# A two-block network on one core: where neighbourhood attention starts beside the recurrence

## The chip, the cores and the metric

One core of a Trainium2 chip runs the whole program. The metric is the device time of one execution in microseconds; the time before is the median of three runs. Engines in the rows: PE is TensorE's matmuls, PEld its weight loads, DVE VectorE, ACT ScalarE, POOL GpSimd, SP SyncE, which issues all DMAs.

## The reference, cut to what matters

Two blocks over 256 tokens of width 1024, all in 32-bit floats. The first block (attention, a state-space mixer, a layer of experts) and the second block's convolutions and feed-forward layers are not touched. The change lies in the even mixer of the second block, which joins two parts:

```python
def even_mixer(h, h_ctx, ...):
    na_q, na_k, na_v, hg_q, hg_ff, hg_fb, hg_i, hg_g = split(h @ w_in)      # and the same of h_ctx
    a_lat = neighbourhood_attention(na_q, na_k, na_v, cna_k, cna_v, rpb)    # 8 heads of 64
    g_lat = hgrn2_mixer(hg_q, (hg_ff, hg_fb), hg_i, hg_g, ...)              # 4 heads of 128
    return concatenate([a_lat, g_lat]) @ w_out

# HGRN2: a recurrence over 8 chunks of 32 tokens, forwards and backwards
o         = qe @ state + (causal part inside the chunk)
new_state = exp(btot) * state + kd.T @ v
# readout, per head
o = o * rsqrt(mean(o * o) + eps) * norm_w * silu(g)
```

Neighbourhood attention of a head: scores of 256 queries against 256 tokens (with a bias) and 256 tokens of context, a softmax, and the weighted sum of values.

## The kernel before, in words

`build` writes one program for each engine (`pe`, `act`, `dve`, `pool`, `sp`). The order on an engine is that of its own Python code; engines meet through semaphores. Code that is to run beside other code is a generator, and `next` puts its next piece into the program at that place, so the order is written out by hand, once for each engine.

Every weight tile of 128x1024 is a unit of a stream. SP loads it, ACT rounds it to a high part (line 1077), DVE subtracts to get a low part (line 1528), and PE makes three products per 128 rows (lines 376 to 378). ACT and DVE call `halves` and `lows` ahead of each wait, so that they work up to `AHEAD` = 3 units in front of PE.

PE's results go to eight PSUM banks. `Banks.take` goes round them in program order of PE and leaves out those that are still held (taken, and not marked full). Whoever takes a bank waits until its last user's data have been read (`is_empty`). So an insertion in PE's order changes which tile later shares a bank with which.

The stage of the change, in PE's order:

1. `recurrence()` (from line 907 on): transposes, the causal part, and then 16 half steps, n = 0 to 7 by direction d. A half step has four state products (`sd`, line 948, only for n < 7) and four output products (line 954) into the banks o0 and o1, which are held until the last half step. DVE does two operations on the state for each (lines 2108 and 2112).
2. `quarters()` (line 968 on): four tiles of weight products are cut into four quarters each, 16 in all, one ahead of each of the 16 half steps. The tiles are named in `QUARTERS`: `("ek", 3)`, the last keys of attention, `("eq", 1)`, the last queries, `("hg", 0)` and `("hg", 1)`, the gate. ACT takes each out of its bank in `tile_out` (line 1340 for eq, 1342 for ek, 1344 for hg with silu).
3. `neighbourhood()`: 16 turns n (head and half of the queries), two yields each, "half turns" 2n and 2n+1. PE: score n (line 877), turned product n-2 (line 868: transposes the probabilities and scales them by a diagonal matrix of reciprocal sums), in the second half valued n-3 (line 887) into a bank `nav` for four turns each. DVE: bias, copy and maximum (lines 2066, 2067, 2069), in the second half the reciprocal and the diagonal of turn n-1 (lines 2074, 2078). ACT: at turns 7, 11, ... the copy of a value tile (line 1402), then copy n-2 of the turned product (line 1407), and the exponential with its sum (line 1414), all ahead of both yields.
4. The heads' readout of the recurrence lies beside attention. DVE copies o out of o0 and o1 (line 2116), ACT squares it (1446), DVE multiplies by the gate (2130), PE sums (`head_mean`, line 999), ACT takes the root (1450), DVE the reciprocal (2134), PE spreads it over two banks os0 and os1 (`head_rows`, line 1008), DVE multiplies (2140), ACT and DVE split the result (1455, 2121). In `act` and `dve` these steps are the generator `heads()`, one `next` per turn; in `pe` they stand at half turns 3 and 7.
5. From half turn 20 on every second half turn carries a half tile of the output projection (`mixer_out`), which needs the readout's results.

Of the kernel before, what the change touches and what calls it, by code (L numbers as in the profile page):

```python
# [155 lines left out]
def build(nc, D, out):  # L156
# [8 lines left out]
    with es:  # L165
# [31 lines left out]
        B = Banks(ps, S)  # L197
# [58 lines left out]
        eq, lists = view(arp, 80, 128, 16), view(scp, 0, 3, 256)  # L256
# [82 lines left out]
        def run(steps):  # L339
            for _ in steps:  # L340
                pass

        VROWS, QUARTERS, HEADS = (0, 3, 6, 9), [("ek", 3), ("eq", 1), ("hg", 0), ("hg", 1)], range(20, 36, 2)

        NORMS = ["n1", "n2", "nc", "l0", "f0", "od", "f1", "fin"]
        RES = {"n2": 0, "l0": 3, "f0": 7, "od": 11, "f1": 14, "fin": 17}
# [21 lines left out]
        def pe(e):  # L370
            t = Eng(e)
# [490 lines left out]
            def neighbourhood():  # L862
                def turned(n):
                    P = take(("nt", n))
                    i = n % 3
                    t.wait_ge(S["n_diag"], n + 1)
                    for k in range(4):
                        last = mm(P[:, k * 128:k * 128 + 128], nP[:, i, k * 128:k * 128 + 128], nD[:, i, :], start=True, stop=True)  # L868
                    last.then_inc(B.full(("nt", n), len(W.units)), 1)

                def scored(n):
                    h, qt = n // 2, n % 2
                    j, b0 = h // 2, 64 * (h % 2)
                    P = take(("ns", n))
                    t.wait_ge(*B.is_empty(("eq", 1)))
                    t.wait_ge(*B.is_empty(("ek", 3)))
                    mm(P[:, :], nq[b0:b0 + 64, j, qt * 128:qt * 128 + 128], nk_[b0:b0 + 64, j, :], start=True, stop=True).then_inc(
                        B.full(("ns", n), len(W.units)), 1)

                def valued(n):  # L880
                    h, qt, i = n // 2, n % 2, n % 3
                    b0 = 64 * (h % 2)
                    P = B[("nav", n // 4)] if n % 4 else take(("nav", n // 4))
                    t.wait_ge(*B.is_empty(("nt", n)))
                    t.wait_ge(*B.is_empty(("nv", 3)))
                    for k in range(4):
                        last = mm(P[b0:b0 + 64, qt * 128:qt * 128 + 128], nv[:, k, h * 64:h * 64 + 64],
                                  nT[i][:, k * 128:k * 128 + 128], start=k == 0, stop=k == 3)
                    if n % 4 == 3:
                        last.then_inc(B.full(("nav", n // 4), len(W.units)), 1)  # L890
                    else:
                        last.then_inc(S["n_part"], 1)
                for n in range(19):
                    if n < 16:
                        scored(n)
                    if 2 <= n < 18:
                        turned(n - 2)
                    yield
                    if n >= 3:
                        valued(n - 3)  # L900
                    yield
# [64 lines left out]
                next(hgr)  # L966
            run(nv_rows)
            W.mark("bias")
            for key in QUARTERS:
                for _ in quarters(key, "ev_" + {"ek": "k", "eq": "q"}.get(key[0], "hg"), key[1] if key[0] == "ek" else 2 * key[1],  # L970
                                  (XA, XC) if key[0] == "ek" else None):
                    next(hgr)


            def cat(k):
# [33 lines left out]
                                  start=True, stop=True)  # L1009
                    last.then_inc(B.full(("os", q), len(W.units)), 1)  # L1010
            heads = (step for i in range(4) for step in mixer_out(i, 1))
            for n, _ in enumerate(neighbourhood()):
                if n == 3:
                    head_mean()
                if n == 7:
                    head_rows()
                if n in HEADS:
                    next(heads)
# [45 lines left out]
        def act(e):  # L1064
# [272 lines left out]
            def tile_out(name, i):  # L1337
                P = bank((name, i))
                if name == "eq":
                    nc.scalar.mul(flat(nq[:, 2 * i:2 * i + 2, :]), P[:, :], 0.125).then_inc(B.empty((name, i)), 1)  # L1340
                elif name == "ek":
                    put(nk_[:, i, :], P[:, :], ACT.Copy).then_inc(B.empty((name, i)), 1)
                else:
                    put(flat(hg[:, 2 * i:2 * i + 2, :]), P[:, :], ACT.Silu).then_inc(B.empty((name, i)), 1)
# [73 lines left out]
            def recurrence():  # L1418
# [15 lines left out]
                for d in range(2):  # L1434
                    P = bank(("s0", d))
                    put(SS[:, d, 0].rearrange("p h v -> p (h v)"), P[:, :], ACT.Copy).then_inc(B.empty(("s0", d)), 1)
                    yield
            run(recurrence())
            for key in QUARTERS:
                tile_out(*key)  # L1440

            def heads():
                for q in range(2):
                    two = slice(2 * q, 2 * q + 2)
                    a.wait_ge(*B.is_empty(("o", q)))
                    put(sq4[:, two], oT[:, two], ACT.Square).then_inc(S["o_sq"], 1)
                yield
                yield
                P = bank("head_stat")
                put(root8, P[:, 0:8], ACT.Sqrt, bias=eps).then_inc(B.empty("head_stat"), 1)  # L1450
                yield
                yield
                for h in range(4):
                    a.wait_ge(*(B.is_empty(("os", h // 2)) if h % 2 else (S["og"], h // 2 + 1)))
                    put(XC[0][:, 4 + h], oT[:, h, :], ACT.Copy).then_inc(S["cat_hh"], 1)
                    if h % 2:
                        yield
            hs = heads()
            for n, _ in enumerate(neighbourhood()):
                if n % 2 == 0:  # L1460
                    next(hs, None)
            run(hs)
# [52 lines left out]
        def dve(e):  # L1515
# [565 lines left out]
            def recurrence():  # L2081
                for s in range(2):
                    for d in range(2):
                        for hf in range(2):
                            lows(B.units[("kt", s, d, hf)] + AHEAD)
                v.wait_ge(*B.is_full(("kt", 1, 1, 1)))
                fill(flat(attT), 0.0).then_inc(own.up(), 1)
                v.wait_ge(own.sem, own.n)
                v.wait_ge(S["ld_hm"], 16)
                for d in range(2):  # L2090
                    for hf in range(2):
                        P = bank(("at", d, hf))
                        nc.vector.copy_predicated(attT[:, d * 8 + hf * 4:d * 8 + hf * 4 + 4, :],
                                                  hm[:, d, :].bitcast(i32).unsqueeze(1).to_broadcast([128, 4, 128]),
                                                  P[:, :].rearrange("p (a b) -> p a b", b=128)).then_inc(B.empty(("at", d, hf)), 1)
                        yield
                for d in range(2):
                    lows(B.units[("s0", d)] + AHEAD)
                for n in range(8):
                    for d in range(2):  # L2100
                        c = n if d == 0 else 7 - n
                        if n < 7:
                            s0, s1 = SS[:, d, n % 2], SS[:, d, (n + 1) % 2]
                            v.wait_ge(S["ebt"], d + 1)
                            v.wait_ge(*B.is_empty(("sd", n - 1, d) if n else ("s0", d)))
                            if n:
                                v.wait_ge(S["o_part"], 2 * (n - 1) + d + 1)
                            tt_(s1, s0, ebt[:, d, :].rearrange("p (h c) -> p h c", c=8)[:, :, c:c + 1].to_broadcast([128, 4, 128]),
                                ALU.mult).then_inc(own.up(), 1)
                            P = bank(("sd", n, d))  # L2110
                            v.wait_ge(own.sem, own.n)
                            tt_(s1, s1, P[:, :].rearrange("p (h v) -> p h v", v=128), ALU.add).then_inc(B.empty(("sd", n, d)), 1)
                        yield
                for q in range(2):
                    v.wait_ge(*B.is_full(("o", q)))
                    copy(flat(oT[:, 2 * q:2 * q + 2, :]), B[("o", q)][:, :]).then_inc(B.empty(("o", q)), 1)
                yield

            def cat_lo(h):
                v.wait_ge(S["cat_hh"], h + 1)  # L2120
# [4 lines left out]
            def heads():  # L2125
                for q in range(2):
                    two = slice(2 * q, 2 * q + 2)
                    v.wait_ge(S["o_sq"], q + 1)
                    v.wait_ge(*B.is_empty(("hg", q)))
                    tt_(oT[:, two], oT[:, two], hg[:, two], ALU.mult).then_inc(S["o_gate"], 1)  # L2130
                yield
                yield
                v.wait_ge(*B.is_empty("head_stat"))
# [12 lines left out]
                    if h % 2:  # L2146
                        yield
            hs = heads()
            for n, _ in enumerate(neighbourhood()):
                if n % 2:  # L2150
                    next(hs, None)
            run(hs)
# [306 lines left out]
```

## Time and profile before

| | |
|---|---|
| median of three runs | 2152.5 us (2150.4 to 2155.31) |
| the profiled execution | 2151.5 us, span 2149.7 us |
| busy: PE, PEld | 98%, 94% of the span |
| busy: DVE, ACT, POOL | 73%, 52%, 12% |
| chain that ended last, by engine | PE 75%, DVE 17%, ACT 4%, DMA 2%, issue 2% |

A row by stretch gives its length, then the busy time of PE, PEld, DVE, ACT and POOL with the number of instructions, then PEclk (TensorE's granted clock as a share of the full 2.4 GHz; 0.50 is 1.2 GHz), the share of the DMA engines' time, and GB/s. A row of a timeline gives start and length in us, engine, line, operation, output and inputs by name with the shape, the count of instructions merged, and in brackets the engine's idle time before it with what ended it. Lengths of neighbouring matmuls overlap a little, so what a piece costs PE is read from one start to the next.

### The profile page before, as it was taken

Reading aid. Unit: us, or ns where it says so; the run is one execution under the profiler, and the core shown is the slowest. Engines: PE = TensorE matmul, PEld = TensorE weight load, DVE = VectorE, ACT = ScalarE, POOL = GpSimd, SP = SyncE. Lnnn points to the kernel's source line nnn. Section 1 sums busy time; section 2 is a strip of 40 time slices with the busy share of each in tenths; the row PEclk is TensorE's granted clock in tenths of the full one; section 3 lists DMA queues with packets and bytes.
Section 4 is the critical chain, followed back from the end, with each engine's and each line's share of the span. In section 5 each row is a group of like instructions: output and inputs, shape, how many; then the busy total and the mean of one; then the engine's idle time right before and its main releaser. Section 6 shows DMA issues by size and latency. Waiting matters only on the chain.

```text
span 2149.7 us, 40331 instructions
## 1 busy us (share of the span) xinstructions
PE 2099.5 (98%) x16798; PEld 2026.2 (94%) x16798; DVE 1565.5 (73%) x2758; ACT 1122.4 (52%) x1745; POOL 261.2 (12%) x256
## 2 busy tenths in 40 slices
PE   7999999999999999999999999999999999999998
PEld 7899998999999999999999999999878999999998
DVE  6877688775999777877777677564455887877764
ACT  5566677545444666654444445463245554445553
POOL 0000000002887445410000000000000000000000
PEclk9999999999999999999999999999989999999999
DMA  5543433567555444447667767322103777655553
GB/s 193 167 135 115 150 118 118 195 217 245 187 187 168 147 145 141 138 165 243 230 236 277 250 226 246 128 89 108 35 20 129 253 248 251 236 193 170 185 181 122
DMA packets 104293, 375.43 MB, mean 175 GB/s; under 512 B 11568, under 2 KB 12208, under 8 KB 103728
## 3 DMA queue, kind: packets, MB, share of 16 engines
q1 hardware_dynamic: 104112, 372.86, 51.6%
q8 instruction: 133, 2.18, 0.4%
q14 instruction: 48, 0.39, 0.1%
HBM read 370.71 MB, written 2.10 MB: 173 GB/s over the span
## 4 chain that ended last, share of the span: by engine, by line
PE 75%; DVE 17%; ACT 4%; DMA 2%; issue 2%; SPq 0%; DVEq 0%; ACTq 0%
PE ps L376 20%; PE ps L377 19%; PE ps L378 19%; DVE wl L1528 3%; PE ps L770 3%; DVE arenap L1870 2%; ACT wh L1077 1%; DVE arena L1671 1%; DMA raw<-in_ada 1%; PE ps L564 1%; PE ps L462 1%; DVE arenap L1835 1%; PE ps L463 1%; PE ps L464 1%; PE ps L868 1%
## 5 line engine op out<-in xcount | busy, mean ns | idle before, releaser
L376 PE MATMUL ps<-xah,wh 128*128 128x256 f32 x2800 | 798.7, 285 | 2.6 <-DVE wl L1528 1.0
L377 PE MATMUL ps<-xal,wh 128*128 128x256 f32 x2800 | 787.5, 281 | 0.0
L378 PE MATMUL ps<-xah,wl 128*128 128x256 f32 x2800 | 786.9, 281 | 0.0
L1077 ACT ACTIVATE wh<-raw 128x1024 fp32r<-128x1024 f32 (+1 forms) x608 | 620.6, 1036 | 296.6 <-PE ps L378 153.6
L1528 DVE TENSOR_TENSOR wl<-raw,wh 128x1024 fp32r<-128x1024 f32 (+2 forms) x548 | 644.6, 1197 | 175.6 <-ACT wh L1077 174.2
L376 PEld LDWEIGHTS ps<-xah,wh 128*128 128x128 f32 x2800 | 528.6, 189 | 13.1 <-issue 5.8
L377 PEld LDWEIGHTS ps<-xal,wh 128*128 128x128 f32 x2800 | 528.8, 189 | 0.5 <-issue 0.2
L378 PEld LDWEIGHTS ps<-xah,wl 128*128 128x128 f32 x2800 | 528.5, 189 | 0.0
L376 PE MATMUL ps<-hh,wh 128*128 128x256 f32 x1024 | 291.1, 284 | 6.8 <-DVE wl L1528 5.1
L377 PE MATMUL ps<-arenar,wh 128*128 128x256 f32 x1024 | 288.7, 282 | 0.0
L378 PE MATMUL ps<-hh,wl 128*128 128x256 f32 x1024 | 288.7, 282 | 0.0
L2255 POOL TENSOR_TENSOR wl<-raw,wh 128x1024 fp32r<-128x1024 f32 x60 | 145.9, 2439 | 553.7 <-ACT wh L1077 553.6
L376 PEld LDWEIGHTS ps<-hh,wh 128*128 128x128 f32 x1024 | 194.2, 190 | 8.5 <-DVE wl L1528 6.5
L377 PEld LDWEIGHTS ps<-arenar,wh 128*128 128x128 f32 x1024 | 194.3, 190 | 0.0
L378 PEld LDWEIGHTS ps<-hh,wl 128*128 128x128 f32 x1024 | 194.1, 190 | 0.0
L2262 POOL TENSOR_SCALAR hh<-cst,scp 128x128 fp32r<-128x128 f32 x192 | 115.1, 618 | 120.2 <-PE ps L770 120.2
L376 PE MATMUL ps<-xfh,wh 128*128 128x256 f32 x416 | 118.1, 284 | 2.3 <-DVE wl L1528 2.1
L378 PE MATMUL ps<-xfh,wl 128*128 128x256 f32 x416 | 117.6, 283 | 0.0
L377 PE MATMUL ps<-xfl,wh 128*128 128x256 f32 x416 | 117.5, 283 | 0.0
L1288 ACT ACTIVATE hh<-arenap 128x256 fp32r<-128x256 f32 x128 | 52.5, 411 | 108.0 <-PE ps L378 108.0
L1910 DVE TENSOR_TENSOR arenar<-arenap,hh 128x256 fp32r<-128x256 f32 x128 | 53.3, 421 | 67.1 <-ACT hh L1288 66.3
L1624 DVE SCALAR_TENSOR_TENSOR scp<-raw,small,scp 128x512 f32<-128x512 f32 x112 | 80.4, 749 | 27.3 <-DMA raw<-in_ada 25.8
(351 smaller groups left out, 3132.2 us busy)
## 6 DMA issues: line engine op xcount, KB each, us to landing
raw<-in_pu SPq DMA_DIRECT2D x128, 512.0 KB, 3.4
raw<-in_pv SPq DMA_DIRECT2D x128, 512.0 KB, 3.7
raw<-in_ada SPq DMA_DIRECT2D x96, 512.0 KB, 4.3
raw<-in_ff_up SPq DMA_DIRECT2D x88, 512.0 KB, 4.2
raw<-in_w_xbc SPq DMA_DIRECT2D x32, 512.0 KB, 3.3
raw<-in_ff_down SPq DMA_DIRECT2D x32, 512.0 KB, 4.0
raw<-in_w_z SPq DMA_DIRECT2D x16, 512.0 KB, 3.2
raw<-in_w_so SPq DMA_DIRECT2D x16, 512.0 KB, 3.9
```

The source lines that it names most:

```text
L376: mm(o, w0, x0, start=start, stop=False, skip_group_check=skip)
L377: mm(o, w0, x1, start=False, stop=False, skip_group_check=skip)
L378: return mm(o, w1, x0, start=False, stop=stop, skip_group_check=skip)
L770: last = mm(P[:, a * 128:a * 128 + 128], o[:, a, :].bitcast(f32), o2[:, a, :], start=True, stop=True)
L1077: put(W.hi(i), W.raw(i), ACT.Copy).then_inc(S["high"], 1)
L1288: put(hh[:, n % 4, :], HA[:, n, :], ACT.Copy).then_inc(S["h_hi"], 1)
L1528: tt_(W.lo(i), W.raw(i), W.hi(i).bitcast(f32), ALU.subtract).then_inc(S["lowV"], 1)
L1624: stt(dst, wv[:, kk, :], by, dst, ALU.mult, ALU.add).then_inc(step[0], 1)
L1870: last = stt(e4[:, :, :, j], p3, float(j), if16[:, tt, s, :, j:j + 1].to_broadcast([128, 8, 16]), ALU.is_equal, ALU.mult)
L1910: tt_(har[n // 32][:, n % 32, :], HA[:, n, :], hh[:, n % 4, :].bitcast(f32), ALU.subtract).then_inc(S["h_lo"], 1)
L2255: nc.gpsimd.tensor_tensor(W.lo(i), W.raw(i), W.hi(i).bitcast(f32), ALU.subtract).then_inc(S["lowG"], 1)
L2262: last = nc.gpsimd.tensor_scalar(ones1[g % 2][:, a, :], iota, lists[:, 0, 4 * g + a:4 * g + a + 1], None, ALU.is_equal)
```

## The change

`QUARTERS` puts the gate's tiles hg 0 and hg 1 ahead of ek 3 and eq 1. PE issues scores 0 and 1 beside the last two half steps, and score 0 waits only for the tiles with its own head's queries and keys. DVE does maxima 0 and 1 and diagonal 0 ahead of the copies of o; ACT does exponentials 0 and 1 ahead of the copy of eq 1. The remaining turns are counted from 3 (PE, ACT) or 4 (DVE). On PE the heads' mean moves from half turn 3 to 5 and the heads' rows from 7 to 9; in `act` and `dve` the first piece of `heads()` now stands ahead of the turns, and one more `yield` follows it.

```diff
-        ... QUARTERS, ... = ..., [("ek", 3), ("eq", 1), ("hg", 0), ("hg", 1)], ...
+        ... QUARTERS, ... = ..., [("hg", 0), ("hg", 1), ("ek", 3), ("eq", 1)], ...
@@ pe: scored(n)
-                    t.wait_ge(*B.is_empty(("eq", 1)))
-                    t.wait_ge(*B.is_empty(("ek", 3)))
+                    t.wait_ge(*B.is_empty(("eq", j // 2)))
+                    t.wait_ge(*B.is_empty(("ek", j)))
@@ pe
+            near, done = neighbourhood(), 0
             for key in QUARTERS:
                 for _ in quarters(key, ...):
+                    if done == 14:
+                        next(near)
+                    elif done == 15:
+                        next(near)
+                        next(near)
                     next(hgr)
+                    done += 1
...
-            for n, _ in enumerate(neighbourhood()):
-                if n == 3:
+            for n, _ in enumerate(near, 3):
+                if n == 5:
                     head_mean()
-                if n == 7:
+                if n == 9:
                     head_rows()
@@ act
+            near = neighbourhood()
             for key in QUARTERS:
+                if key == QUARTERS[3]:
+                    for _ in range(3):
+                        next(near)
                 tile_out(*key)
@@ act: heads(), behind the squares, and dve: heads(), behind the gate
+                yield
                 yield
                 yield
@@ act
             hs = heads()
-            for n, _ in enumerate(neighbourhood()):
+            next(hs)
+            for n, _ in enumerate(near, 3):
                 if n % 2 == 0:
                     next(hs, None)
@@ dve: recurrence()
-                for n in range(8):
+                for n in range(7):
...
+                for _ in range(4):
+                    next(near)
                 for q in range(2):
                     v.wait_ge(*B.is_full(("o", q)))
                     copy(flat(oT[:, 2 * q:2 * q + 2, :]), B[("o", q)][:, :]).then_inc(B.empty(("o", q)), 1)
@@ dve
             hs = heads()
-            for n, _ in enumerate(neighbourhood()):
+            next(hs)
+            for n, _ in enumerate(near, 4):
                 if n % 2:
                     next(hs, None)
```

## Rows read from the trace of the kernel before

**Rows 1.** Busy time by stretch; PEclk is TensorE's granted clock, 1.00 full.
```profile
1552.00:1576.00 24.00, 21.59 (x90) 15.17 (x90) 12.40 (x31) 11.45 (x21) 0.00 (x0) 0.72 0.03 11
```

**Rows 2.** Order of time, PE, around the change: start, length, instruction, idle before.
```profile
1549.47 0.97 PE L954 MATMUL ps<-arena 128*128 128x32 f32 x8
...
1551.79 0.97 PE L954 MATMUL ps<-arena 128*128 128x32 f32 x8
1553.10 1.98 PE L877 MATMUL ps<-arena 64*128 64x512 f32 x4 [0.34 <-DVE arena L2116]
1557.15 3.58 PE L999 MATMUL ps<-J,arena 128*128 128x1 f32 x16 [2.08 <-ACT arena L1446]
1560.66 2.07 PE L877 MATMUL ps<-arena 64*128 64x512 f32 x2
1562.66 2.07 PE L868 MATMUL ps<-sc,arena 128*128 128x128 f32 x8
...
1568.67 1.80 PE L887 MATMUL ps<-arena 128*64 128x128 f32 x8
1570.40 2.05 PE L1008 MATMUL ps<-cst,small 128*128 128x128 f32 x16
1572.38 1.12 PE L877 MATMUL ps<-arena 64*128 64x512 f32 x2
1573.43 1.16 PE L868 MATMUL ps<-sc,arena 128*128 128x128 f32 x8
1574.52 1.09 PE L887 MATMUL ps<-arena 128*64 128x128 f32 x8
1575.54 1.12 PE L877 MATMUL ps<-arena 64*128 64x512 f32 x2
```

**Rows 3.** Busy time by microsecond, columns as in rows 1.
```profile
957.00:958.00 1.00, 0.14 (x2) 0.00 (x0) 0.21 (x1) 0.82 (x2) 0.00 (x0) 1.00 0.09 33
958.00:959.00 1.00, 0.12 (x1) 0.15 (x2) 1.00 (x3) 1.00 (x2) 0.00 (x0) 1.00 0.85 262
...
1556.00:1557.00 1.00, 0.00 (x0) 0.00 (x0) 0.00 (x0) 1.00 (x3) 0.00 (x0) 0.75 0.00 0
...
1570.00:1571.00 1.00, 1.00 (x8) 0.83 (x8) 0.00 (x0) 0.99 (x2) 0.00 (x0) 0.92 0.00 0
```

**Rows 4.** The page: the splits of weights on DVE, count, busy, mean ns.
```profile
L1528 DVE TENSOR_TENSOR wl<-raw,wh 128x1024 fp32r<-128x1024 f32 (+2 forms) x548 | 644.6, 1197 | 175.6 <-ACT wh L1077 174.2
```

**Rows 5.** The same stretch on DVE.
```profile
1552.35 1.29 DVE L2116 COPY arena<-ps 128x512 f32<-128x512 f32 x2 [4.51 <-PE ps L954]
...
1554.26 0.42 DVE L2066 TENSOR_TENSOR arena<-ps,arena 128x256 f32<-128x256 f32 x1
...
1555.05 0.69 DVE L2069 TENSOR_REDUCE sc<-arena 128x1 f32<-128x512 f32 x1
1557.13 1.29 DVE L2130 TENSOR_TENSOR arena<-arena 128x512 f32<-128x512 f32 x2 [1.40 <-ACT arena L1446]
...
1567.68 0.20 DVE L2134 RECIPROCAL small<-small 128x8 f32<-128x8 f32 x1 [3.04 <-ACT small L1450]
...
1575.12 0.29 DVE L2078 TENSOR_SCALAR sc<-cst,sc 128x128 f32<-128x128 f32 x1
1575.32 0.87 DVE L2140 SCALAR_TENSOR_TENSOR arena<-arena,pcol,ps 128x256 f32<-128x256 f32 x2
```

**Rows 6.** The same stretch on ACT.
```profile
1551.99 0.60 ACT L1344 ACTIVATE arena<-ps 128x512 f32<-128x512 f32 x1 [5.23 <-PE ps L378]
...
1555.77 0.72 ACT L1414 ACTIVATE arena<-arena,sc 128x512 f32<-128x512 f32 x1 [1.89 <-DVE sc L2069]
...
1556.49 1.13 ACT L1446 ACTIVATE arena<-arena 128x512 f32<-128x512 f32 x2
...
1566.08 1.28 ACT L1450 ACT_TABLE_LOAD   x1
1567.38 0.27 ACT L1450 ACTIVATE small<-ps,small 128x8 f32<-128x8 f32 x1
```

More of the change, by code:

```diff
@@ L341, in run @@
                 pass
-        VROWS, QUARTERS, HEADS = (0, 3, 6, 9), [("ek", 3), ("eq", 1), ("hg", 0), ("hg", 1)], range(20, 36, 2)
+        VROWS, QUARTERS, HEADS = (0, 3, 6, 9), [("hg", 0), ("hg", 1), ("ek", 3), ("eq", 1)], range(20, 36, 2)
         NORMS = ["n1", "n2", "nc", "l0", "f0", "od", "f1", "fin"]
@@ L2117, in recurrence @@
                 yield
+            near = neighbourhood()
             def cat_lo(h):
@@ L2130, in heads @@
                     tt_(oT[:, two], oT[:, two], hg[:, two], ALU.mult).then_inc(S["o_gate"], 1)
+                yield
                 yield
```

## The prediction

> **What bounds the kernel now.** I read the page first: PE is busy in 98% of the span and DVE in 73%, so only places where PE waits, or runs slowly, can give time back. The place the diff touches is the seam between the gated recurrence and neighbourhood attention. The stretch view [rows 1] says what is wrong there: in 24 us PE is busy for 21.59 us, and its mean granted clock is 0.72. The timeline of PE [rows 2] gives the reason. After the recurrence's last matmuls (1551.79) PE waits 0.34 us for bank o0, which DVE still copies out, runs two scores (two records each) up to 1555.08, and then stands 2.08 us before the heads' mean (line 999), because ACT squares o (line 1446) behind the first exponential. In that idle time the clock falls from full to half, in the microsecond with a mean of 0.75 [rows 3]; it is full again early in the one with 0.92. From 1557.15 on, a score takes 2.00 us instead of 1.05 and a turned product 2.0 instead of 1.09 (starts [rows 2]).
>
> So the seam costs, against a PE that never stops: 0.34 + 2.08 = 2.4 us idle, and the half clock. From 1557.15 to 1572.38 there are 15.2 us of work. At full clock it is: mean 1.8 (half of 3.5), two scores at 1.05, two turned at 1.09, one valued at 1.02, head rows 1.98, together 9.1. The half clock costs 6.2 us, the seam 8.6. That is the most this change can win, 0.4% of the kernel.
>
> **The change part by part.** Half turn k below is the k-th yield of the neighbourhood generator (turn n has 2n and 2n+1). All times are on the axis of the trace.
>
> *Order of the quarter tiles.* The same products and the same seven weight units; the first four are split before the quarters begin, ek's and eq's follow beside the products of hg, in gaps that ACT and DVE have there as before. 0.0 us. If that cover were gone, PE would wait for one split on DVE, 1.2 us [rows 4]. The bias load stands before the same seventh unit, so it stays early.
>
> *Scores 0 and 1.* They slip between PE's last pieces. From 1549.47 to 1551.79 there lie one o product and one quarter tile, 2.32 us [rows 2], which I part as 0.81 and 1.51. Score 0 begins at 1549.47, o ends 1551.33, the last quarter 1552.84, score 1 ends 1553.9, the last o 1554.7, score 2 ends 1555.8. No wait: by the rotation of the eight banks (o0 and o1 are still held) the scores now take banks emptied long ago. The 0.34 us goes. DVE finds score 0 at 1550.6; a maximum is ready 1.48 us after its score (1554.26 to 1555.74 [rows 5]), an exponential 0.8 us later (0.72 [rows 6] and the read of its sum). Maximum 1 is out at 1555.45, diagonal 0 at 1555.9 [rows 5].
>
> *Wait 1, new.* The rotation gives turned product 0 the bank of the tile eq 1. ACT now empties that tile behind exponential 1: 1555.5 + 0.8, then 0.60 for the copy [rows 6], done at 1556.85. PE stands from 1555.8 to 1556.9: **1.1 us**. Behind it on ACT are the squares (1.13 [rows 6]), ready at 1558.0, just when turned 0 ends. So the heads' mean in its new place waits for nothing: the 2.08 us goes.
>
> *Wait 2, new.* The mean and the rows move by two half turns on PE (3 to 5, 7 to 9). On ACT the root moves from half turn 4 to 8, on DVE the reciprocal from 5 to 9: two generator steps are gone to the front and one yield is added, and each step is two half turns. So the root now stands behind exponential 4, whose score is PE's last but two. At full clock: score 4 ends 1564.0, maximum 1565.5, ACT copies turned 2 (until 1565.75), exponential 1566.6, table load 1.28, root 0.27 [rows 6], reciprocal 0.20 [rows 5]: 1568.35. PE has turned 2 and valued 1 to do, until 1566.1, and then stands **2.3 us** (between 2.0 and 2.5, by how the copy falls). Before, the same chain was ready at 1567.88, 2.5 us ahead of line 1008.
>
> The Trainium skill, "ScalarE: Activation LUTs", section "What ACT_TABLE_LOAD costs", gives a switch of tables about 2.66 us, the load and a drain behind it. In this trace the root starts 0.02 us after a load of 1.28 us has ended [rows 6]; by the page wait 2 would be 3.7 us instead of 2.3, and the sum below +4.9 us. I go by the row.
>
> *Wait 3, new.* The rotation of the banks gives the second value tile of attention (valued 4, turn 7) the bank of the second head rows. DVE empties that bank in line 2140, which has moved from half turn 11 to 15, behind turn 7's maximum and diagonal. From score 7's end: maximum 1.48, reciprocal and diagonal 0.45, line 2140 0.87 [rows 5], 2.8 us, against 1.09 us of PE's turned 5: 1.7 us at least. ACT adds to it: its two copies of o (0.8) now stand ahead of the copy of value tile 0, for which DVE's queue waits ahead of maximum 7. I take **2.2 us**, between 1.7 and 2.9.
>
> Waits: 1.1 + 2.3 + 2.2 = 5.6 us instead of 2.4. So the change moves PE's idle time apart, and more than doubles it; what it can win lies in the clock.
>
> *The clock.* The rows show no simple price. PE stood 1.7 us in 957 to 959 [rows 3], between dense products, and the clock stayed full. At 1555.08 it stood 2.08 us and the clock fell, after two scores that use 64 rows of the array. In the new order the stretch from 1552.84 to 1559.8 holds two scores, one o product with 32 columns a matmul, one turned product, the mean with one column in each of its matmuls, and 1.1 us idle: hardly more work for PE than in the stretch where it fell. I take it that the clock falls there again, near 1556.5, and is back at about 1570.1 as before. Then: turned 0 from 1556.9 to 1558.9, mean to 1562.4, score 3 to 1564.4, turned 1 to 1566.4, valued 0 to 1568.15, score 4 to 1570.15, turned 2 and valued 1 at full clock to 1572.25. The root's chain from score 4 ends 4.1 us after it, at 1574.25, so wait 2 is 2.0 us; head rows to 1576.2. Score 5 starts at 1576.2 where it started at 1575.54: 0.7 us late. With wait 3 and an uncertain 0.6 for ACT's and DVE's fuller turn 7, the sum is **+3.5 us** (0.7 + 2.2 + 0.6). Ends of this case: +1.9 if the clock is back earlier (at 1566.7), +5.5 if later or with wait 3 at its upper bound.
>
> The profiled execution took 2151.5 us (span 2149.7), 1.0 below the median of the three runs, 2152.5. I put the sum on the median: 2156.0.
>
> **The rivals.**
> 1. *The clock stays full at the seam.* For it: PE's longest gap there shrinks from 2.08 to 1.1 us, and 1.7 us cost nothing at 957. Against: the thin matmuls around it. Then 6.2 us of half clock go, and idle time grows by 3.2: -3.0 us, 2149.5.
> 2. *The clock falls a second time, in wait 2 or wait 3 (slower).* Place: 1566 to 1568, or turn 7. Both gaps are as long as the one that let it fall before, and nothing dense stands beside wait 3. Price: one more half-clock stretch of 3.4 to 6.8 us (half or a quarter of the 13.6 us from 1556.5 to 1570.1 [rows 3]), half of that lost, 1.7 to 3.4, on top of +3.5: about +6.5, 2159.0. It decides as soon as PE's wait before the head rows or before valued 4 is over 2 us. The Trainium skill, "TensorE: Matmul & The Clock Gate", section "A second HAM failure mode: psum-queue depth-cycling", says that a PE which keeps stopping shortly between groups of matmuls, as it goes round the PSUM banks, can let its clock swing between the levels. By that rule this rival is the likeliest outcome, at its 2159.0; the trace of before agrees once (2.08 us) and disagrees once (1.7 us).
> 3. *The new waits are not there or are short*, because an engine is quicker than I have it or the bank order differs: 8.6 less 1.1 to 3 us, about -6.5, 2146.0. For it: a large part of the 8.6 is real. Against: the half turns are written in the code.
> 4. *Nothing to see:* gain and waits cancel, 2152.5.
>
> **How the numbers follow.** About 0.2% (4.3 us) is what a measurement of this kernel can tell from no change. Forecast 35%, rival 1 20%, rival 2 27%, rival 3 10%, rival 4 8%. Faster by over 0.2% (under 2148.2): rival 3 and a part of rival 1, 0.15. Slower (over 2156.8): rival 2 but for a little, and the upper third of the forecast, 0.38. The rest, 0.47, is within. Range: from rival 1's 2149.5 less 1 to rival 2's 2159 plus 2.5, 2148.5 to 2161.5; what is left out is rival 3 and the tail of rival 2.
>
> **What would show each step.** PE has no wait between the last quarter and score 2. ACT's copy of eq 1 ends before turned 0 starts, with a PE wait of about 1.1 us released by ACT's line of that copy. The line of the head rows waits for DVE's reciprocal, 2 us or more. Valued 4 waits for DVE's line 2140 (its number after), about 2 us. PEclk between 1553 and 1576 is at 0.5 for about 13 us. I am wrong if it stays at 1.0 there, if head rows or valued 4 wait for nothing, or if the clock is at 0.5 anywhere in turns 5 to 10.

## The result and the profile after

| | changed | before | ratio, 95% interval |
|---|---|---|---|
| first comparison (6 runs each) | 2157.88 us | 2152.32 us | 1.0027 (1.0015 to 1.0039) |
| second, later (10 and 27 runs) | 2157.28 us | 2152.22 us | 1.0031 (1.0019 to 1.0043) |
| profiled execution, span | 2155.5 us | 2149.7 us | |

The change costs 5 to 6 us by the medians, 0.3% (by the two intervals together, 3 to 9 us). The forecast was 2156.0, +3.5. Of all executions one, of kernel 2 below, took 5224 us; its ratio leaves it out, and the median of 2147.90 given there would be 2147.51 without it.

All three new waits are there. PE after the change, in order of time (to compare with [rows 2]; this kernel reached its quarter tiles 1.3 us earlier, at 1496.34 instead of 1497.66):

```profile
1551.80 1.12 PE L877 MATMUL ps<-arena 64*128 64x512 f32 x2
1552.85 1.08 PE L954 MATMUL ps<-arena 128*128 128x32 f32 x8
1553.86 1.12 PE L877 MATMUL ps<-arena 64*128 64x512 f32 x2
1555.82 1.75 PE L868 MATMUL ps<-sc,arena 128*128 128x128 f32 x8 [0.84 <-ACT arena L1347]
1557.35 3.41 PE L1006 MATMUL ps<-J,arena 128*128 128x1 f32 x16
1560.69 2.07 PE L877 MATMUL ps<-arena 64*128 64x512 f32 x2
...
1566.55 1.12 PE L877 MATMUL ps<-arena 64*128 64x512 f32 x2
...
1568.69 1.09 PE L887 MATMUL ps<-arena 128*64 128x128 f32 x8
1572.06 2.64 PE L1015 MATMUL ps<-cst,small 128*128 128x128 f32 x16 [2.28 <-DVE small L2152]
1574.63 2.07 PE L877 MATMUL ps<-arena 64*128 64x512 f32 x2
...
1580.35 1.12 PE L877 MATMUL ps<-arena 64*128 64x512 f32 x2
...
1584.56 1.16 PE L868 MATMUL ps<-sc,arena 128*128 128x128 f32 x8
1587.95 1.09 PE L887 MATMUL ps<-arena 128*64 128x128 f32 x8 [2.23 <-DVE arena L2158]
1588.97 1.12 PE L877 MATMUL ps<-arena 64*128 64x512 f32 x2
```

The waits of 0.34 and 2.08 us are gone. In their place stand 0.84 us before turned product 0, released by ACT's copy of eq 1 (L1347), 2.28 us before the head rows (L1015), released by DVE's reciprocal (L2152), and 2.23 us before valued 4, released by the products of the readout (L2158). Why the first is there and the second is so long can be read on ACT. The copy of eq 1 starts behind exponential 1 (the read of its sum). Exponential 4, the table load and the root follow each other directly:

```profile
1555.10 0.19 ACT L1421 ACTIVATION_READ_ACCUMULATOR arena<-arena,sc 128x1 f32 x1
1555.19 0.58 ACT L1347 ACTIVATE arena<-ps 128x512 f32<-128x512 f32 x1
...
1569.30 0.71 ACT L1421 ACTIVATE arena<-arena,sc 128x512 f32<-128x512 f32 x1
1569.91 0.19 ACT L1421 ACTIVATION_READ_ACCUMULATOR arena<-arena,sc 128x1 f32 x1
1570.12 1.28 ACT L1462 ACT_TABLE_LOAD   x1
1571.41 0.27 ACT L1462 ACTIVATE small<-ps,small 128x8 f32<-128x8 f32 x1
```

The third can be read on DVE, where value tile 0 (L2074), maximum 7 and its diagonal stand ahead of the second pair of products:

```profile
1584.92 0.42 DVE L2074 TENSOR_TENSOR xcl<-ps,xch 128x256 fp32r<-128x256 f32 x1 [0.75 <-ACT xch L1409]
1585.26 0.42 DVE L2079 TENSOR_TENSOR arena<-ps,arena 128x256 f32<-128x256 f32 x1
...
1586.83 0.29 DVE L2091 TENSOR_SCALAR sc<-cst,sc 128x128 f32<-128x128 f32 x1
1587.03 0.87 DVE L2158 SCALAR_TENSOR_TENSOR arena<-arena,pcol,ps 128x256 f32<-128x256 f32 x2
```

PEclk, last column but two, by microsecond, answers to [rows 3]:

```profile
1556.00:1557.00 1.00, 1.00 (x7) 1.00 (x7) 0.71 (x3) 0.80 (x2) 0.00 (x0) 0.60 0.00 0
...
1566.00:1567.00 1.00, 1.00 (x5) 0.56 (x4) 0.00 (x0) 0.10 (x2) 0.00 (x0) 0.78 0.00 0
...
1573.00:1574.00 1.00, 1.00 (x8) 1.00 (x7) 0.00 (x0) 0.00 (x0) 0.00 (x0) 0.64 0.00 0
...
1580.00:1581.00 1.00, 1.00 (x5) 0.47 (x3) 0.00 (x0) 0.99 (x2) 0.00 (x0) 0.95 0.00 0
```

A mean of 0.60 in a microsecond is a fall after its first fifth. So the clock is at half from 1556.2 to 1566.4 and again from 1573.3 to 1580.1, just after the long wait before the head rows: 17.1 us instead of 13.7. The second fall is the one of rival 2. The last wait, 2.23 us before valued 4, is not followed by one.

### The profile page after: what moved, and what is told of

The parts are those of the page before. It is cut to its first block, busy times and chain, and to the rows that moved or that the text cites. A ratio compares the mean times of both kernels' runs of the same rounds, so it can differ in the third digit from the quotient of the medians.

```text
span 2155.5 us, 40333 instructions
## 1 busy us (share of the span) xinstructions
PE 2099.1 (97%) x16798; PEld 2025.3 (94%) x16798; DVE 1565.8 (73%) x2758; ACT 1123.0 (52%) x1745; POOL 261.1 (12%) x256
## 4 chain that ended last, share of the span: by engine, by line
PE 73%; DVE 17%; ACT 5%; DMA 2%; issue 2%; SPq 0%; DVEq 0%; ACTq 0%
PE ps L376 19%; PE ps L377 19%; PE ps L378 19%; DVE wl L1541 3%; PE ps L770 3%; DVE arenap L1883 2%; ACT wh L1084 2%; DVE arena L1684 1%; DMA raw<-in_ada 1%; PE ps L564 1%; PE ps L462 1%; DVE arenap L1848 1%; PE ps L463 1%; PE ps L464 1%; DVE arenap L1843 1%
```

## The experiments

The median moves by whatever the clock does in other stages as well: by the mean clocks of the profiles, 26 to 38 us at half clock lie outside the seam. So I also read one length in each profile: from the first quarter tile to the start of score 11, behind the seam. "Idle" is the sum of PE's waits of over 0.15 us in it, "half" the time at half clock, "added" the time of products that compute nothing, and "rest" is length - idle - half/2 - added. Every profile also has one wait of 0.93 us before score 11; it is the same in all and stays in "rest".

One profile is one execution. The last column takes all of them: the time that a whole execution lost to the clock, (1 - its mean granted clock) x its span, as the mean over a kernel's executions, and in brackets the same of the kernel before measured beside it. It is worked out from clocks given to three digits; the standard error is about 0.4 us for the kernel before and 0.5 to 1.3 for the others.

| | length | idle | half | added | rest | lost, all executions (before) |
|---|---|---|---|---|---|---|
| before | 99.24 | 2.42 | 13.7 | 0 | 90.0 | 22.9, 23.6 and 23.7 |
| changed | 104.52 | 5.35 | 17.1 | 0 | 90.6 | 26.7 (23.7) |
| root earlier | 95.09 | 0.84 | 6.8 | 0 | 90.9 | 22.7 (22.9) |
| and eq 1 first | 93.18 | 0.20 | 3.4 | 0 | 91.3 | 19.1 (22.9); once more 19.3 (23.7) |
| order alone | 97.94 | 2.42 | 10.2 | 0 | 90.4 | 23.4 (22.9) |
| before, gap filled | 94.35 | 0.34 | 0.0 | 3.2 | 90.8 | 18.2 (22.9) |
| products late | 105.12 | 3.07 | 23.9 | 0 | 90.1 | 25.1 (23.6) |
| changed, rows' gap filled | 104.35 | 3.07 | 13.7 | 3.9 | 90.5 | 23.1 (23.6) |
| mean later | 97.95 | 2.10 | 10.2 | 0 | 90.8 | 25.0 (23.6) |
| eq 1 first, mean filled | 97.13 | 0.00 | 10.2 | 1.3 | 90.7 | 17.8 (23.6) |
| the same once more | 95.60 | 0.00 | 6.8 | 1.3 | 90.9 | 17.9 (23.7) |

Changed and eq 1 first were profiled twice (second time 104.53 with 17.1, and 91.59 with 0.0 of half clock; rest 90.6 and 91.4). The rest stays within 1.4 us, so idle time and half clock explain nearly all of the differences at this place. Half/2 is a rough price: before, the clock fell 0.64 us ahead of the end of the idle time (1556.51, against 1557.15), and half clock in idle time costs nothing, so the rest of before is nearer 90.3.

All executions of the second comparison agree with the table: the changed kernel's mean is 5.9 us above the other's (2158.0 and 2152.1), of which 3.0 is the clock and 2.9 is not, and the profiles have 2.93 us more idle time.

**1. Root earlier** (the changed kernel without its added yields):

```diff
@@ act: heads(), behind the squares, and dve: heads(), behind the gate
-                yield
                 yield
                 yield
```

> The changed kernel, but ACT's and DVE's heads() have no added yield, so the root stands behind exponential 3 instead of 4 and line 2158's two pairs of products (the old 2140) at half turns 11 and 13 instead of 13 and 15. Theory (the loss is the two waits that the half turns make, 2.28 us before the head rows and 2.23 us before valued 4, and the second fall of the clock in the first of them, 6.8 us at half clock = 3.4 us): both waits are gone, the clock falls once at the seam, 8 us less than the changed kernel, about 2150. Rival A (the loss is in starting the scores early, by the wait for the tile eq 1 and a longer mean): the time stays within 2 us of the changed kernel, 2156 to 2158. Rival B (the clock's swings have nothing to do with these waits): only 4.5 us come back, 2153.4, and the clock still falls twice.

Measured: 2151.31 us, before 2151.57, ratio 1.0000 (0.9991 to 1.0009). PE of this kernel at the head rows and at valued 4:

```profile
1569.37 1.09 PE L887 MATMUL ps<-arena 128*64 128x128 f32 x8
1570.38 2.05 PE L1015 MATMUL ps<-cst,small 128*128 128x128 f32 x16
...
1579.73 1.16 PE L868 MATMUL ps<-sc,arena 128*128 128x128 f32 x8
1580.82 1.09 PE L887 MATMUL ps<-arena 128*64 128x128 f32 x8
```

Neither has a wait, and the clock falls once. One `yield` in each of two engines' programs is the whole loss of the change. Rivals A and B are out. The profile's seam is 4.2 us shorter than before, which the times do not show. Most of that is the profile's half clock, 6.8 us instead of 13.7, and over all executions the clock takes as much as before (22.7 and 22.9 us): this profile had luck with the clock. What the early scores win in idle time, 1.6 us less 0.9 of rest, is within the interval.

**2. Eq 1 first** (on top of 1):

```diff
@@ act
                 if key == QUARTERS[3]:
-                    for _ in range(3):
-                        next(near)
+                    next(near)
+                    next(near)
                 tile_out(*key)
+            next(near)
```

> As the kernel with the root earlier, and ACT copies the tile eq 1 between exponentials 0 and 1 instead of behind both. Theory: turned 0 waits only for its diagonal, the 0.84 us wait before it shrinks to about 0.1 us; the squares are ready no sooner, so PE waits up to 0.8 us before the heads' mean instead. The gain over the kernel with the root earlier is 0 to 0.8 us: about 2149.8. Rival (the wait before turned 0 is what lets the clock fall at 1556): the clock stays full at the seam and 4 to 6 us more come back, 2144 to 2146.

Measured: 2146.41 us, before 2151.57, ratio 0.9980 (0.9970 to 0.9990); once more 2147.90 against 2152.22, 0.9982 (0.9973 to 0.9991). The rival came closer in time, though its clock stayed full in one of two profiles only. Just 0.6 us of idle time went, yet the ratio is 0.2% better than the last one's. The clock accounts for most of it: in the two profiles 3.4 and 0.0 us at half clock are left, and over all executions 19.1 us are lost instead of 22.7.

```profile
1555.18 1.13 PE L868 MATMUL ps<-sc,arena 128*128 128x128 f32 x8
1556.35 1.95 PE L1006 MATMUL ps<-J,arena 128*128 128x1 f32 x16
1558.23 1.12 PE L877 MATMUL ps<-arena 64*128 64x512 f32 x2
1559.55 2.01 PE L868 MATMUL ps<-sc,arena 128*128 128x128 f32 x8 [0.20 <-DVE sc L2091]
```

Turned 0 and the mean follow score 2 with hardly a gap, and the clock (a turned product is 2.01 us again) falls only behind the mean and score 3. In the second profile it does not fall here at all.

**3. Order alone** (the kernel before with the new `QUARTERS`):

> The kernel before with the order of the quarter tiles of the change alone (hg 0, hg 1, ek 3, eq 1), scores where they were. Theory: nothing, 2152.3 within 1.5 us; PE has the same 0.34 and 2.08 us waits at the seam. Rival (a wait for a late weight split or for the last tiles of attention moves into the quarters): 1 to 3 us slower, with a wait inside the 16 quarters.

Measured: 2152.62 us, before 2151.57, 1.0006 (0.9997 to 1.0015), waits of 0.34 and 2.08 us as before. Nothing, as expected.

**4. The gap before the mean filled, in the kernel before:**

```diff
@@ pe: head_mean()
                 P = take("head_stat")
+                keep(P, 14)
```

> The kernel before with 14 products of the identity with itself (128 columns, into unused columns of the mean's bank) ahead of the wait for the heads' mean, some 1.9 us of dense work in its 2.08 us gap. Theory (6.2 us of the seam are half clock, caused by that gap): the clock stays full, scores take 1.05 us, and the time falls by 5 to 6 us less what DVE and ACT then hold up, 2146 to 2149. Rival (the thin matmuls of the mean with one column each let the clock fall even without a gap): the clock falls at the seam all the same, a step later at most, and the time is within 2 us of 2152.3.

Measured: 2148.70 us, before 2151.57, ratio 0.9985 (0.9976 to 0.9994).

```profile
1557.19 3.39 PE L476 MATMUL ps<-cst 128*128 128x128 f32 x28
1560.42 1.84 PE L1000 MATMUL ps<-J,arena 128*128 128x1 f32 x16
1562.20 1.12 PE L877 MATMUL ps<-arena 64*128 64x512 f32 x2
1563.25 1.16 PE L868 MATMUL ps<-sc,arena 128*128 128x128 f32 x8
```

Useless work in the gap makes the kernel faster: score and turned product behind it take 1.05 and 1.09 us, and the clock never leaves 1.00 in this seam; over all executions 18.2 us are lost to it instead of 22.9. I had the 14 products at 1.9 us; they take 3.2 (two records each), so 1.15 us of them is past the gap's end. So the gap is what let the clock fall in this seam: filled with dense products, it did not. That a gap is needed for a fall is not shown, and kernel 8 below speaks against it.

**5. Products late** (as 1, but the added yield behind the root and the reciprocal): the wait of valued 4 by itself.

```diff
@@ act and dve: heads(), against the changed kernel
-                yield
                 yield
                 yield
                 ... the root; the reciprocal ...
                 yield
                 yield
+                yield
```

> The changed kernel with the added yield of heads() in ACT and DVE put behind the root and the reciprocal instead of ahead of them: the root stands behind exponential 3, the two pairs of products stay at half turns 13 and 15. Theory (the two waits are separate; the one before the head rows, with the second fall of the clock, costs 5.7 us, the one before valued 4 costs 2.2): the wait before the head rows is gone, valued 4 still waits 1.7 to 2.3 us, one fall of the clock; the time is 2.2 us above the kernel with the root earlier (2151.3), about 2153.5. Rival (a gap of 2.2 us in thin work always lets the clock fall): it falls again behind valued 4 and the time is 2155 to 2157.

Measured: 2155.17 us, before 2152.51, ratio 1.0017 (1.0006 to 1.0028).

```profile
1583.04 1.16 PE L868 MATMUL ps<-sc,arena 128*128 128x128 f32 x8
1586.43 1.36 PE L887 MATMUL ps<-arena 128*64 128x128 f32 x8 [2.23 <-DVE arena L2158]
1587.72 2.07 PE L877 MATMUL ps<-arena 64*128 64x512 f32 x2
1589.72 2.08 PE L868 MATMUL ps<-sc,arena 128*128 128x128 f32 x8
```

PE has the 2.23 us before valued 4 and then runs at half clock (a score 2.00 us again). Against kernel 1 (1.0000) the one wait costs 0.17% or 3.7 us, 1.4 more than its length; the intervals are too wide to tell that surplus by time, but the profile shows the fall. The rival came true here: this gap too can let the clock fall. It does not always, since the changed kernel's two profiles have the same wait and no fall.

**6. Head rows' gap filled, in the changed kernel:**

```diff
@@ pe: head_rows()
                 for q in range(2):
                     P = take(("os", q))
+                    if q == 0:
+                        keep(P, 17)
                     t.wait_ge(S["rstd8"], 1)
```

> The changed kernel with 17 products of the identity with itself ahead of the wait for the head rows' reciprocal, 2.1 us of dense work in the 2.28 us gap; all three waits keep their ends. Theory (the second fall of the clock, 6.8 us at half clock, costs 3.4 us by itself, and idle time calls it): one fall at the seam, none at 1573; the head rows start when they did, and the time is 3.0 us less, about 2154.9. Rival (the second fall costs nothing, since DVE and ACT are late at that place anyway): the clock stays full and the time stays at 2157.9.

Measured: 2155.74 us, before 2152.51, ratio 1.0025 (1.0011 to 1.0039), which overlaps the changed kernel's own: undecided by time.

```profile
1568.65 4.06 PE L476 MATMUL ps<-cst 128*128 128x128 f32 x34
1572.55 1.95 PE L1017 MATMUL ps<-cst,small 128*128 128x128 f32 x16
...
1585.19 1.47 PE L887 MATMUL ps<-arena 128*64 128x128 f32 x8 [2.23 <-DVE arena L2160]
1586.59 2.07 PE L877 MATMUL ps<-arena 64*128 64x512 f32 x2
```

The 17 products take 3.9 us, 1.6 more than the gap, so the head rows did not start when they had. In the profile the clock does not fall there, as the theory has it, but it falls behind valued 4 (at 1585.7), where it had stayed full in the changed kernel.

**7. Mean later** (on top of 2):

```diff
@@ pe
-                if n == 5:
+                if n == 6:
                     head_mean()
```

> The kernel with eq 1 copied between the exponentials (2146.4), and PE's heads' mean at half turn 6 instead of 5, behind score 3 and turned 1. Theory (what lets the clock fall there is thin work side by side: scores, the last o product, and the mean's one-column products with a short wait): with denser pieces around the mean the clock stays full in most runs, 1 to 2 us less, 2144.5 to 2145.5. Rival (ACT's root then waits for the mean and holds up the copy of turned 2): a new wait of 0.5 to 1 us before valued 1 or the head rows, the clock as before, 2147.

Measured: 2151.92 us, before 2152.51, 1.0002 (0.9993 to 1.0012). Both were wrong.

```profile
1558.64 1.12 PE L877 MATMUL ps<-arena 64*128 64x512 f32 x2
1561.86 1.16 PE L868 MATMUL ps<-sc,arena 128*128 128x128 f32 x8 [2.10 <-DVE sc L2091]
```

Turned 1 now stands where the mean was and waits 2.10 us for DVE's diagonal 1, which stands behind the copies of o, the gate and maximum 2. In kernel 2 the mean covers that time. Its place was right. Behind this wait the clock falls for 10.2 us in the profile.

**8. Mean filled** (on top of 2):

```diff
@@ pe: head_mean()
                 P = take("head_stat")
+                keep(P, 6)
```

> The kernel with eq 1 copied between the exponentials (2146.4), with 6 products of the identity ahead of the heads' mean, 0.8 us of dense work where PE has almost no gap. Theory (one stretch of 3.4 us at half clock is left there and costs 1.7 us): the clock stays full, 1.7 us come back and 0.8 are paid, 2145.5. Rival (the mean itself is thin enough): the clock falls all the same and the time is 0.8 us more, 2147.2.

Measured: 2147.74 us, before 2152.51, ratio 0.9971 (0.9961 to 0.9982).

```profile
1562.76 1.12 PE L877 MATMUL ps<-arena 64*128 64x512 f32 x2
1563.81 1.32 PE L868 MATMUL ps<-sc,arena 128*128 128x128 f32 x8
1565.06 1.97 PE L887 MATMUL ps<-arena 128*64 128x128 f32 x8
```

The theory's "the clock stays full" did not hold in the profile: it falls at 1564.7 for 10.2 us, and PE has no wait of over 0.15 us ahead of it in the seam. In the second profile of this kernel (below) it falls twice, at 1557.9 and 1564.7, for 3.4 us each, again without such a wait. Both profiled executions took more than their medians (2150.98 and 2152.20 us), and over all executions this kernel loses least to the clock, 17.8 and 17.9 us.

The last three runs, all on one chip:

> The changed kernel once more, beside the two below on one chip. Theory: 5.6 us above the kernel before, 2157 to 2159. Rival (its first six runs were unlucky with the clock): 2154 or less.

> The root earlier and eq 1 copied between the exponentials, once more. Theory: 4 to 5 us under the kernel before, 2147 to 2148 where that takes 2152. Rival (the first result was the chip's): within 2 us of it.

> The same with 6 products of the identity ahead of the heads' mean, once more. If these keep the clock up often enough, it is 1 to 2 us under the one without them; if they only cost their 0.8 us, it is 0 to 1 us above it.

Measured: changed 2157.28, eq 1 first 2147.90, mean filled 2147.02 us; ratios 1.0031, 0.9982, 0.9977 (0.9968 to 0.9986). The two without the yields beat both the kernel before and the changed one, by 4 to 5 us and by 9 to 10 us. Between themselves nothing can be told.

## Why the prediction was right, and where it was not

- *Order of the tiles, 0.0 us:* right (kernel 3).
- *No wait up to score 2:* right.
- *Wait 1, 1.1 us:* 0.84. *Wait 2, 2.3 us:* 2.28. *Wait 3, 2.2 us:* 2.23. Together 5.35 instead of 5.6 (5.3 in the case that the sum takes, with wait 2 at 2.0), and each was released by the instruction named. The places were read from the half turns in the code and from the bank rotation, the lengths from single rows.
- *The clock, "falls there again, near 1556.5, and is back at about 1570.1":* this is the step that failed. It fell at 1556.2, was back at 1566.4, and fell again at 1573.3 for 6.8 us. The forecast kept half clock at 13.6 us, the profiles have 17.1 twice; 1.7 us more. That is rival 2, which I had at 27%; the prediction's own sign of being wrong, half clock in turns 5 to 10, came true from score 5 (1574.63) on. Rival 2's price was over-stated (+6.5; measured +5.6 and +5.1), because the first stretch came out 3.4 us shorter than before.
- The sum by the table: idle +2.9, half clock +1.7, rest +0.6, 5.3 us in the seam. The forecast's 0.7 and 2.2 are the same +2.9 of idle time, with nothing for the clock. That +3.5 came out near the measured +5.6 is in part luck: 0.6 of it was not there, and the second fall, 6.8 us at half clock, was half made good by the shorter first one.
- The rest, between 90.0 and 91.4, is not explained in full. Some 0.3 us of the +0.6 is the rough price of half clock. A part may be the cutting of scores and output products apart: one output product and one quarter tile took 2.32 us before and 2.51 (1549.29 to 1551.80) after. That was not tested by itself, and it can't be why kernel 2 has 0.7 more than the changed kernel, whose products are cut the same way.
- *"The uncertain 0.6 for a fuller turn 7"* was not there as a wait.
- Rival 1 (clock full at the seam, -3.0) did not come in the changed kernel's profiles, but it is what kernel 2 had in one of two.
- ACT's root starts 0.01 us after its table load has ended (1571.41), and wait 2 is 2.28 us long. The 3.7 us that would follow from the Trainium skill, "ScalarE: Activation LUTs", section "What ACT_TABLE_LOAD costs", are not seen.
- PE stops three times in the seam, and the clock swings down twice, behind the first two stops. The Trainium skill, "TensorE: Matmul & The Clock Gate", section "A second HAM failure mode: psum-queue depth-cycling", speaks of such swings in a PE that keeps stopping shortly between groups of matmuls; the trace of the changed kernel agrees. The falls in kernel 8, at 1564.7 and in the second profile at 1557.9, have no such stop ahead of them.

What stays open: the profiles are one or two executions each, while the clock's falls differ from one execution to the next (order alone has the same waits as before, but 10.2 us at half instead of 13.7). How often each wait makes it fall was not counted; the last column of the table gives only what the clock took in a whole execution.

## What to carry to other kernels

Where several engines' programs are woven by hand, moving one piece on one engine means counting each engine's steps anew: here one engine's step was half a turn and the others' a whole one, and one `yield` too many cost 6 us. After every insertion go round the PSUM banks again and ask who now empties the next user's bank, and behind what. A wait of TensorE has to be priced with the clock behind it: between the changed kernel and kernel 2 the seam's profiles differ by 11.3 us: 5.2 of idle time and 6.8 for 13.7 us more at 1.2 GHz, less 0.7 of rest. And a single profile says little about the clock: look at the mean granted clock of all executions before a fall that came or stayed away is put down to an edit.

## What was not expected of the hardware

Work that computes nothing made the kernel before faster by 0.15% (ratio 0.9985), since in the profile it kept the granted clock at 1.00 through a gap of 2.08 us, even though it ran 1.15 us past its end. And a gap's length alone does not say whether the clock falls: 2.23 us before valued 4 let it fall in kernels 5 and 6 and not in the changed kernel's two profiles, 0.84 us with scores and one-column products beside it was followed by a fall in each profile that had it, and in both profiles of kernel 8 the clock fell (for 10.2 us, and twice for 3.4) though PE had no wait over 0.15 us in the seam.
